# Block-major cache rows for a compressed-branch product, with the position embedding as an extra column

## What is computed

```
idx    = arange(n_cmp)[:, None] * 16 + arange(32)[None, :]      # n_cmp = 15 blocks of 32 rows, stride 16
blocks = rows[:, idx] + pos_emb[:, None, :]
flat   = blocks.transpose(0, 1, 3, 2, 4).reshape(B, n_cmp, KV, 32 * 64)
return gelu(flat @ w1) @ w2                                      # once for keys, once for values
```

## Time and profile before

| | us |
|---|---|
| median of 3 runs | 2906.92 |
| lowest and highest run | 2904.03, 2912.76 |
| span of the profiled execution (its own time) | 2918.1 |

### The profile page before, as it was taken

One profiled execution on the slowest core, in us unless ns is written; L12 is line 12 of the kernel. 1 busy time (PEld: TensorE's weight loads), 2 busy tenths in 40 slices (PEclk: granted clock), 3 DMA queues, 4 the chain that ended last, 5 costly groups with the idle time before them and its releaser, 6 DMA issues. The chain is left out here.

```text
span 2918.1 us, 45487 instructions
## 1 busy us (share of the span) xinstructions
PE 2805.5 (96%) x17763; PEld 2651.7 (91%) x17763; DVE 1577.8 (54%) x1539; ACT 472.0 (16%) x1106; POOL 788.6 (27%) x579
## 2 busy tenths in 40 slices
PE   7999999999999999999898998979999999999997
PEld 6999999799999969998586777969999999999996
DVE  4555555355555564453655544555565565555555
ACT  2110000111000130000523542031100000000002
POOL 1321332133233620000433101633323322322353
PEclk9999999999999999999656777979999999999998
DMA  6555555355555445663331113535455555545542
GB/s 178 154 153 157 155 138 148 103 151 153 156 153 139 121 106 145 153 147 87 130 97 33 48 47 94 137 85 146 136 165 145 145 143 158 150 133 163 152 131 84
DMA packets 734087, 380.73 MB, mean 130 GB/s; under 512 B 65402, under 2 KB 729722, under 8 KB 733386
## 3 DMA queue, kind: packets, MB, share of 16 engines
q1 hardware_dynamic: 733754, 378.60, 47.2%
q10 hardware_dynamic: 272, 1.36, 0.1%
HBM read 370.60 MB, written 13.38 MB: 132 GB/s over the span
## 5 line engine op out<-in xcount | busy, mean ns | idle before, releaser
L292 PE MATMUL bank<-xh_before,wh_before 128*128 128x320 f32 x2112 | 657.2, 311 | 11.3 <-DVE wl_before L310 11.3
L293 PE MATMUL bank<-xl_before,wh_before 128*128 128x320 f32 x2112 | 655.0, 310 | 0.0
L294 PE MATMUL bank<-xh_before,wl_before 128*128 128x320 f32 x2112 | 655.0, 310 | 0.0
L292 PE MATMUL bank<-xh_after,wh_after 128*128 128x320 f32 x1664 | 521.5, 313 | 22.1 <-DVE wl_after L310 13.6
L308 DVE CAST wh_before<-raw 128x2048 fp32r<-128x2048 f32 (+1 forms) x196 | 219.2, 1119 | 596.6 <-PE bank L294 565.4
L293 PE MATMUL bank<-xl_after,wh_after 128*128 128x320 f32 x1664 | 518.5, 312 | 0.0
L294 PE MATMUL bank<-xh_after,wl_after 128*128 128x320 f32 x1664 | 518.4, 312 | 0.0
L310 DVE TENSOR_TENSOR wl_before<-raw,wh_before 128x2048 fp32r<-128x2048 f32 (+1 forms) x196 | 464.0, 2368 | 6.7
L308 DVE CAST wh_after<-raw 128x2048 fp32r<-128x2048 f32 (+1 forms) x168 | 184.9, 1101 | 436.0 <-PE bank L294 435.5
L310 DVE TENSOR_TENSOR wl_after<-raw,wh_after 128x2048 fp32r<-128x2048 f32 (+1 forms) x168 | 409.4, 2437 | 5.8
L292 PEld LDWEIGHTS bank<-xh_before,wh_before 128*128 128x128 f32 x2112 | 398.7, 189 | 13.3 <-issue 8.6
(11 more groups left out here) (232 smaller groups left out, 3436.0 us busy)
## 6 DMA issues: line engine op xcount, KB each, us to landing
raw<-in_w_ffn_in SPq DMA_DIRECT2D x176, 1024.0 KB, 5.8
raw<-in_w_ffn_out SPq DMA_DIRECT2D x128, 704.0 KB, 4.8
raw<-in_w_in SPq DMA_DIRECT2D x36, 1024.0 KB, 5.7
raw<-in_w_in SPq DMA_DIRECT2D x16, 512.0 KB, 5.2
raw<-in_w_out SPq DMA_DIRECT2D x16, 512.0 KB, 4.3
raw<-in_w_out SPq DMA_DIRECT2D x64, 128.0 KB, 3.9
proj<-in_cache_cmp_kv SPq DMA_DIRECT2D x64, 64.0 KB, 2.5
raw<-in_state_gla SPq DMA_DIRECT2D x8, 512.0 KB, 4.5
```

The costliest lines, as they stand in the source:

```text
L292: pe.matmul(out, L.wh[a][:, w], hi[:, k], start=(k == 0), stop=False)
L293: pe.matmul(out, L.wh[a][:, w], lo[:, k], start=False, stop=False)
L294: last = pe.matmul(out, L.wl[a][:, w], hi[:, k], start=False, stop=(k == nk - 1))
```

## The change

`R` becomes [128, 8 j, 16 i, 33 c], with m = 8 i + j and column c = 4 b + k for sample b and head k. Column 32 holds the position embedding. For row pair l the moving operand is `R[:, l % 8, l // 8 : l // 8 + 15]`, 15 x 33 = 495 elements in one run. The result in bank 6 has 33 values for each block; of the column 32 only that of block 0 is used, as the bias. The matmuls of L397, bank 7's part and the semaphore `biased` are gone. GpSimd clears column 32 once, at the end of the first half of the first chunk; ScalarE writes the position values of n into it (`place_pos`). Its copies out of the banks scatter over `R`, and the gelu permutes on its way out, so that `L.hid` is laid out as before. The buffers behind `R` move up by 128 elements.

```diff
-        self.R = flat[:, 5120:9216].rearrange("p (b k m) -> p b k m", b=NB, k=KV)
-        self.w1 = flat[:, 9216:11264].rearrange("p (l m) -> p l m", m=P)
+        self.R = flat[:, 5120:5120 + 8 * 16 * 33].rearrange("p (j i c) -> p j i c", i=16, c=33)
+        self.w1 = flat[:, 9344:11392].rearrange("p (l m) -> p l m", m=P)
...
@@ tensor_hidden
         pe.wait_ge(self.w_in, 16 * (n + 1))
-        pe.wait_ge(self.pos_taken, 1)
+        pe.wait_ge(self.pos_placed, n + 1)
         if n:
             pe.wait_ge(self.acted, 1)
-            pe.wait_ge(self.bias_taken, 1)
-        for l in range(LT):
-            mm = pe.matmul(L.bank[7][:, 0:1], self.w1[:, l], self.posT[:, n * LT + l:n * LT + l + 1],
-                           start=(l == 0), stop=(l == LT - 1))
-        mm.then_inc(self.biased, 1)
         pe.wait_ge(self.taken, NB * (n + 1))
         for l in range(LT):
-            mm = pe.matmul(L.bank[6][:, 0:NB * KV * NC], self.w1[:, l],
-                           self.R[:, :, :, l:l + 8 * (NC - 1) + 1:8].rearrange("p b k n -> p (b k) n"),
+            mm = pe.matmul(L.bank[6][:, 0:NC * 33], self.w1[:, l],
+                           self.R[:, l % 8, l // 8:l // 8 + NC].rearrange("p n c -> p (n c)"),
                            start=(l == 0), stop=(l == LT - 1))
@@ scalar
             act.activation(self.posT, L.bank[6][:, 0:32], ACT.Copy).then_inc(self.pos_taken, 1)
+            act.wait_ge(self.cleared, 1)
+            act.wait_ge(self.pos_taken, 1)
+            self.place_pos(act, 0)
         for j in (2 * h, 2 * h + 1):
             act.wait_ge(self.turned, j + 1)
             if j == NB:
                 act.wait_ge(self.hidden, 1)
-            act.activation(self.R[:, j % NB].rearrange("p k m -> p (k m)"), L.bank[2 + j % 4][:], ACT.Copy
+                self.place_pos(act, 1)
+            b = j % NB
+            act.activation(self.R[:, :, :, b * KV:(b + 1) * KV].rearrange("p j i k -> p k i j"),
+                           L.bank[2 + j % 4][:].rearrange("p (k i j) -> p k i j", k=KV, j=8), ACT.Copy
                            ).then_inc(self.taken, 1)
...
+    def place_pos(self, act, n):
+        act.activation(self.R[:, :, 0:2, 32], self.posT[:, n * 16:(n + 1) * 16].rearrange("p (i j) -> p j i", i=2),
+                       ACT.Copy).then_inc(self.pos_placed, 1)
+
+    def gpsimd(self, pool):
+        pool.memset(self.R[:, :, :, 32], 0.0).then_inc(self.cleared, 1)
@@ scalar_hidden
-        act.wait_ge(self.biased, n + 1)
-        act.activation(L.cmp_bias[:, n:n + 1], L.bank[7][:, 0:1], ACT.Copy).then_inc(self.bias_taken, 1)
+        act.wait_ge(self.hidden, n + 1)
+        act.activation(L.cmp_bias[:, n:n + 1], L.bank[6][:, 32:33], ACT.Copy).then_inc(self.bias_taken, 1)
         act.wait_ge(self.bias_taken, n + 1)
-        act.wait_ge(self.hidden, n + 1)
-        act.activation(L.hid[n][:, 0:NB].rearrange("p b k n -> p (b k n)"), L.bank[6][:, 0:NB * KV * NC],
+        act.activation(L.hid[n][:, 0:NB].rearrange("p b k n -> p n (b k)"),
+                       L.bank[6][:, 0:NC * 33].rearrange("p (n c) -> p n c", c=33)[:, :, 0:NB * KV],
                        ACT.Gelu_apprx_tanh, bias=L.cmp_bias[:, n:n + 1]).then_inc(self.acted, 1)
@@ ffn, gpsimd
+                    if side and c == 0:
+                        side.gpsimd(pool)
```

More of the change, by code:

```diff
@@ L326, in __init__ @@
         flat = L.proj[:].rearrange("p k t -> p (k t)")
-        self.R = flat[:, 5120:9216].rearrange("p (b k m) -> p b k m", b=NB, k=KV)
-        self.w1 = flat[:, 9216:11264].rearrange("p (l m) -> p l m", m=P)
-        self.rows = [flat[:, 11264 + 512 * i:11776 + 512 * i].rearrange("p (k a d) -> p k a d", k=KV, a=2)
+        self.R = flat[:, 5120:5120 + 8 * 16 * 33].rearrange("p (j i c) -> p j i c", i=16, c=33)
+        self.w1 = flat[:, 9344:11392].rearrange("p (l m) -> p l m", m=P)
+        self.rows = [flat[:, 11392 + 512 * i:11904 + 512 * i].rearrange("p (k a d) -> p k a d", k=KV, a=2)
                      for i in range(4)]
-        self.pos = flat[0:32, 13312:13440]
-        self.posT = flat[:, 13440:13472]
+        self.pos = flat[0:32, 13440:13568]
+        self.posT = flat[:, 13568:13600]
         self.rows_in = [L.sem(f"blocks_rows_in{i}") for i in range(4)]
         self.w_in, self.table_in, self.pos_in = (L.sem("blocks_" + x) for x in ("w_in", "table_in", "pos_in"))
-        self.turned, self.taken, self.hidden, self.acted, self.pos_turned, self.pos_taken = (
-            L.sem("blocks_" + x) for x in ("turned", "taken", "hidden", "acted", "pos_turned", "pos_taken"))
-        self.biased, self.bias_taken = L.sem("blocks_biased"), L.sem("blocks_bias_taken")
+        self.turned, self.taken, self.hidden, self.acted, self.pos_turned, self.pos_taken, self.pos_placed = (
+            L.sem("blocks_" + x) for x in ("turned", "taken", "hidden", "acted", "pos_turned", "pos_taken",
+                                           "pos_placed"))
+        self.bias_taken, self.cleared = L.sem("blocks_bias_taken"), L.sem("blocks_cleared")
     def load_w1(self, sp, n):
```

## The result

| | before | changed |
|---|---|---|
| median, 16 runs each (us) | 2913.92 | 2899.52 |
| lowest and highest | 2903.43, 2925.03 | 2881.28, 2902.65 |
| span of the profiled execution | 2918.1 | 2883.0 |
| ratio, 95% interval | | 0.9938, 0.9923 to 0.9952 |

The change makes the kernel 0.62% faster, 18 us (14 to 22). I had forecast 23.8 us off a median of 2906.9, so 2883.1, and 2899.5 is 16.4 above that. Of these, 7.0 are the kernel before: its median is 2913.9 over 16 runs, not the 2906.9 of three. The other 9.4 are gain that I forecast and the medians do not show, and some 6 of them are missing from the means as well.

The account below looks back on a forecast made before the run. TensorE, busy 96% of the span, was taken to bound the kernel, with L402 waiting for its stepped reads. Savings of 16.8 and 7.0 us sum to 23.8, off a median of 2906.9: 2883.1 us, range 2875 to 2893.

Parts of the forecast that it names:

- The pace: New product on TensorE: 495 contiguous columns take 0.414 us a record, 13.25 us for sixteen instructions.
- L402's pace did not follow the clock: Old hidden product: 4 records in 2 us at clock 0.50 and at 1.00, so it waits for its reads.
- The first group: End of the first FFN's second chunk: bias product gone, product shorter, ending at 526.99 instead of 543.82; saves 16.8 us.
- the term of the copies: ScalarE's last two copies ahead of the first product, stepping by 33 elements: no extra cost, 0.595 us a copy.
- The other end: First group's copies at twice their cost: the pair ends 1.1 to 1.2 us later and the saving is 15.7.
- The nearest row: Profile row chosen for the stepped copies' cost: this copy itself, same engine and element count, at 0.595 us.
- The second group: Start of the projection: 9.65 us come through behind the LayerNorm, less 2.7 lost to a clock of 0.50; saves 7.0.
- The rival in which the clock stays up: Second group: clock stays at 1.00 behind the LayerNorm, nothing charged; 26.5 us saved, 2880.4 us; chance 0.15.
- The small pieces: Memset, other copies, position column, bias copies and permuted gelu: covered by slack or waits; counted as nothing.
- The sum: Whole kernel: 16.8 + 7.0 = 23.8 us saved, taken off the median of 2906.9, giving 2883.1 us.
- The range: Whole kernel: 2875 to 2893 us, to take in the clock staying up, dearer copies and the runs' spread.

Follow-up runs that it names:

- e1: The changed kernel with the block-major layout alone: 32 columns a block, no position column, bias matmuls kept; median 2901.78 us, ratio 0.9942.
- e2: The changed kernel with the position column alone: R stays sample by sample, operand steps by 8, bias matmuls gone; median 2918.28 us, ratio 0.9998.
- e7: The changed kernel with unneeded matmuls filling TensorE's waits behind the two LayerNorms that feed a matmul; median 2895.91 us, ratio 0.9922.
- e8: As e7, with VectorE instead of ScalarE making the last sample's copy ahead of the first product; median 2889.87 us, ratio 0.9920.
- e11: The changed kernel with 17 unneeded matmuls (2.49 us) ahead of the linear attention; mean 2893.0 us.
- e13: The changed kernel with 23 unneeded matmuls (3.4 us) ahead of the linear attention; mean 2898.3 us.
- e15: The kernel before with 12 unneeded matmuls (1.76 us) ahead of the linear attention; mean 2921.0 us, ratio 1.0027.
- e9: The changed kernel with 6 unneeded matmuls (0.88 us) ahead of the linear attention; mean 2894.1 us.
- e12: The changed kernel once more, unaltered, beside the padded ones as their reference; median 2898.60 us, ratio 0.9942.

## Why the prediction was wrong, and where it was right

- **The pace** was right: 0.417 us a record against 0.414, and the stride is the cause (e1, e2). That L402's pace did not follow the clock was right too, and e1 shows that contiguous reads do follow it.
- **The first group**: 16.8 us forecast, 15.8 measured. The missing 1.0 us is the term of the copies. I took no extra cost for the step of 33 elements; a copy takes 1.10 us instead of 0.595, the wait is 1.67 us instead of 0.8. The other end that I kept, by TensorE's ratio for stepped reads, said 1.1 to 1.2 us and was the right one, and the Trainium skill (SBUF — State Buffer, the note on cachelines) had pointed there. The nearest row was not the copy with contiguous writes but the fact that stepping costs.
- **The second group**: 7.0 forecast, 7.1 measured (from the first transpose of the last half chunk to the first matmul of the linear attention: 370.65 before, 363.53 after). The second unit starts 28.4 us after the product, as forecast, and the clock took 5.48 - 2.94 = 2.5 us of it (2.7 forecast). The rival in which the clock stays up is false: in the changed kernel the clock was already falling between 1036 and 1038, while TensorE was still walking behind VectorE with waits of 0.25 to 0.61 us, and with these waits filled it stays up (e7). The idle-gap reading of the Trainium skill (TensorE: Matmul & The Clock Gate, "Why this matters for your kernels"), by which the rival would have held, disagrees with the trace here. The wait of 2.75 us for L310 in e1 fits that section of the Trainium skill better.
- **The small pieces**: the copies at the first half-chunk end finish at 200.2 us, and no unit waits. The slow copies are paid once only, at 512.9.
- **The sum** of these terms was 23.8, and 23.0 is what the two groups give in the profiles and 23.5 what the kernels give without the attention stages. What failed is the step from the sum to the time: "as the terms are differences inside it, I take them off the median: 2906.9 - 23.8". It went wrong twice. It assumed that every stage behind the groups takes the same time on average. The attention stages take 389 to 412 us in the profiles for the same instructions, by the clock that they are granted, and with them the means differ by 17.5 us instead of 23.5: 6 us of the gain are lost there, and why stays open. And it took the median of three runs for that of the kernel before, 7.0 us too low.
- **The range** failed by the same two errors together. Either alone would have left the time inside it: 2913.9 - 23.8 is 2890.1, and 2906.9 less the 14.4 by which the medians differ is 2892.5. I had the spread of single runs (2904.0 to 2912.8) from three runs, where 16 spread from 2903.4 to 2925.0. The profile could have warned me: its span of 2918.1 was above all three, and the clock line has seven slices between 5 and 7 tenths in the middle.

## What to carry to other kernels

A moving operand of fp32 that steps by 32 bytes cost TensorE twice its time here (0.886 us a record against 0.417) and was worth a new layout. It is worth one elsewhere, if the engine that writes the layout pays its own doubled copies under cover; look at the one place where they are bare. Ask of each shortened stretch what walks behind it: here the second group's own work became 17.7 us shorter, and 7.1 us of that came through; the rest went into a LayerNorm and its clock. And where the clock changes often in a later stage, compare stretches of the profile and not single totals, for such a stage moved the total of single executions here by about as much as the change did (23 us between profiles).

## What the hardware showed beyond what I expected

- Writes with a step of 33 fp32 elements cost ScalarE 1.10 us for 512 elements instead of 0.595, and VectorE's copy took 1.03 us (e8). The gelu with a step of 15 elements takes 1.10 us for 480 instead of 0.66.
- The same 1,787 matmul records of the attention stages took 388.6 us at a mean clock of 0.71 (e11) to 412.4 us at 0.65 (e13).
- Twelve matmuls of no use went with a mean 6.5 us higher in one kernel (e15), and 6 to 17 of them with means 2.7 to 5.1 us lower in another (e9 to e11 against e12). No run shows why.
- In three executions of one kernel the clock fell behind the same LayerNorm at three places within 4 us of each other (1036 to 1042 us), so a loss to the clock of a few us differs from execution to execution.
